# Sums of weight quarters made by accumulating transfers, and paired blocks moved, in the FFNs of a two-block model on one core

## The reference, cut to what matters

```python
x = x + (jax.nn.silu(h2 @ ffn_w1[l]) * (h2 @ ffn_w3[l])) @ ffn_w2[l]
```

## Time and profile before

| | before |
|---|---|
| median of 3 executions | 1043.04 us (1043.03 to 1043.26) |
| span of the profiled execution | 1041.3 us |
| PE busy | 1033.9 us, 99% of the span |
| DVE busy | 843.5 us, 81% |
| ACT busy | 593.8 us, 57% |
| POOL busy | 21.6 us, 2% |
| TensorE's granted clock | full in all 40 slices |

### The profile page before, as it was taken

The page is one execution under the profiler, slowest core; times in us unless marked ns, Lnnn a source line. Parts: engine busy times, 40 slices in busy tenths (PEclk is TensorE's granted clock), DMA queues, the critical chain, the costliest instruction groups (busy, mean ns, idle before and its releaser), DMA issues.

```text
span 1041.3 us, 13328 instructions
## 1 busy us (share of the span) xinstructions
PE 1033.9 (99%) x4884; PEld 841.5 (81%) x4884; DVE 843.5 (81%) x1366; ACT 593.8 (57%) x897; POOL 21.6 (2%) x30
## 2 busy tenths in 40 slices
PE   9999999999999999999999999999999999999998
PEld 7877778888888888788888888787777888888887
DVE  6877889797868987896887788989978878878684
ACT  6845474655646646655656564638656446466462
POOL 0221000000000000000000000000000000000000
PEclk9999999999999999999999999999999999999999
DMA  8762478382456534683743653544444468739243
GB/s 278 228 206 83 128 249 270 122 277 87 142 187 187 180 134 142 216 283 126 246 140 96 221 169 122 158 151 154 147 160 135 148 189 258 242 122 303 85 153 107
DMA packets 135706, 182.97 MB, mean 176 GB/s; under 512 B 12588, under 2 KB 82730, under 8 KB 135514
## 3 DMA queue, kind: packets, MB, share of 16 engines
q1 hardware_dynamic: 134130, 178.36, 53.2%
q0 software_dynamic: 1104, 3.21, 1.2%
q10 hardware_dynamic: 408, 0.56, 0.2%
HBM read 181.03 MB, written 1.05 MB: 175 GB/s over the span
## 4 chain that ended last, share of the span: by engine, by line
PE 92%; DVE 5%; ACT 2%; issue 1%; DVEq 0%; ACTq 0%
PE ps L2169 13%; PE ps L2174 13%; PE ps L2170 13%; PE ps L2186 7%; PE ps L2187 7%; PE ps L2191 7%; PE ps L2309 4%; PE ps L2311 4%; PE ps L2314 4%; PE ps L2152 3%; PE ps L2154 3%; PE ps L2153 3%; DVE wlo L1175 1%; PE ps L2259 1%; PE ps L2242 1%; PE ps L2733 1%
## 5 line engine op out<-in xcount | busy, mean ns | idle before, releaser
L1175 DVE TENSOR_TENSOR wlo<-raw,whi 128x1024 fp32r<-128x1024 f32 (+1 forms) x290 | 349.4, 1232 | 28.8 <-ACT whi L631 27.1
L631 ACT ACTIVATE whi<-raw 128x1024 fp32r<-128x1024 f32 (+1 forms) x290 | 295.5, 1053 | 106.9 <-DMA raw<-in_ffn_w_in 33.1
L2169 PE MATMUL ps<-whi,ath 128*128 128x512 f32 (+1 forms) x688 | 274.5, 400 | 2.2 <-ACT whi L631 0.7
L2170 PE MATMUL ps<-whi,atl 128*128 128x512 f32 (+1 forms) x688 | 266.4, 388 | 0.0
L2174 PE MATMUL ps<-wlo,ath 128*128 128x512 f32 (+1 forms) x688 | 182.9, 388 | 0.0
L2169 PEld LDWEIGHTS ps<-whi,ath 128*128 128x128 f32 x688 | 129.3, 188 | 35.6 <-issue 5.9
L2174 PEld LDWEIGHTS ps<-wlo,ath 128*128 128x128 f32 x688 | 128.2, 188 | 27.4 <-DVE wlo L1175 0.6
L2170 PEld LDWEIGHTS ps<-whi,atl 128*128 128x128 f32 x688 | 129.4, 188 | 24.7 <-issue 0.5
L2186 PE MATMUL ps<-whi,brh 128*128 128x512 f32 x272 | 106.5, 392 | 0.0
L2187 PE MATMUL ps<-whi,brl 128*128 128x512 f32 x272 | 105.9, 389 | 0.0
L1189 DVE TENSOR_TENSOR wlo<-work,whi 128x1024 fp32r<-128x1024 f32 x84 | 98.7, 1220 | 4.5 <-ACT whi L648 4.5
(11 more groups left out here) (380 smaller groups left out, 1415.4 us busy)
## 6 DMA issues: line engine op xcount, KB each, us to landing
raw<-in_ffn_w_in SPq DMA_DIRECT2D x112, 256.0 KB, 3.5
raw<-in_w_in SPq DMA_DIRECT2D x104, 256.0 KB, 2.9
raw<-in_ffn_w SPq DMA_DIRECT2D x100, 256.0 KB, 3.5
raw<-in_ffn_w_out SPq DMA_DIRECT2D x88, 256.0 KB, 3.5
work<-in_ffn_w_in SPq DMA_DIRECT2D x64, 256.0 KB, 4.8
raw<-in_a_w_in SPq DMA_DIRECT2D x48, 256.0 KB, 4.3
raw<-in_b_w_in SPq DMA_DIRECT2D x48, 256.0 KB, 3.1
work<-in_ffn_w SPq DMA_DIRECT2D x32, 256.0 KB, 4.6
```

Source lines behind the costliest of these rows:

```text
L631: a_(unit_view(whi, slot, w), unit_view(raw, slot, w), ACT.Copy).then_inc(hi_ready, 1)
L1175: v_.tensor_tensor(unit_view(wlo, slot, w), unit_view(raw, slot, w), unit_view(whi, slot, w), ALU.subtract).then_inc(lo_ready, 1)
L2169: mm(ps[bk + apart * t][:, 0:w], ath[:, k, t * P:(t + 1) * P], rh[:, kk, :], start=k == 0, stop=False)
L2170: mm(ps[bk + apart * t][:, 0:w], atl[:, k, t * P:(t + 1) * P], rh[:, kk, :], start=False, stop=False)
```

## The change

The pairs move to blocks 5 and 6, and 9 and 10, so the second pair ends the FFN: its last turns and down units take the place of those of the plain block 10, and the turn of one `hid` stands in the middle of the last product. The signs of the scheme change, so that t1 = b11 + b12, t3 = b12 + b22, t2 = b22 + t1 and t4 = b21 + t2; `rneg`, the negative of `rstd`, takes up the sign. DVE makes t2 and t4 only. t1 and t3 are made in their tiles by transfers: one quarter is loaded, and a second transfer adds the other quarter to it (`accum_op`). The quarters are loaded by POOL (`ffn_parts`) in a fixed chain of waits, not by SP: five whole tiles and two added ones a pair, each 4 transfers of 256 KB. The first pair's chain starts at the FFN's second unit, and the second pair's waits tile by tile until the first pair's low halves are made; its last load is b22.

```diff
@@ -56,7 +56,7 @@
-PAIRED = (4, 8)
+PAIRED = (5, 9)
...
@@ -69,8 +69,11 @@
-            plan += [("up", j + 2, c) for c in range(4)]
-            plan += [("down", j + b, k) for b in range(2) for k in range(2)]
+            if j + 2 < FB:
+                plan += [("up", j + 2, c) for c in range(4)]
+                plan += [("down", j + b, k) for b in range(2) for k in range(2)]
+            else:
+                plan += [("down", j, k) for k in range(2)]
...
@@ -87,21 +90,9 @@
-PARTS = [f"{b}_{i}" for b in ("b11", "b12", "b22", "b21") for i in range(2)]
-_p0 = plan_at("pair", 0, "b11", 0)
-PART_LOADS = {}
-for _i, _name in enumerate(PARTS):
-    PART_LOADS.setdefault(6 + 2 * _i, []).append((0, _name))
-for _i, _name in enumerate(PARTS[:4]):
-    PART_LOADS.setdefault(_p0 + 7, []).append((1, _name))
-for _i, _name in enumerate(PARTS[4:]):
-    PART_LOADS.setdefault(_p0 + 18 + _i, []).append((1, _name))
 SUMS = ["a0", "a1", "s1", "s2", "s3", "s4", "l1", "l2", "l3", "l4"]
 for _k in range(len(PAIRED)):
-    SUMS += [f"{_k}_{_t}_{_i}" for _t in ("t1", "t3", "t2", "t4") for _i in range(2)] + [f"{_k}_{_c}" for _c in ("c22", "c11", "c21")]
+    SUMS += [f"{_k}_{_t}_{_i}" for _t in ("t2", "t4") for _i in range(2)] + [f"{_k}_{_c}" for _c in ("c22", "c11", "c21")]
...
@@ -500,14 +494,6 @@
-                    for pair, name in PART_LOADS.get(i, ()):
-                        b, h = name.split("_")
-                        if pair:
-                            sp.wait_ge(lo_ready, u0 + plan_at("pair", 0, "t3" if b == "b12" else b, int(h)) + 1)
-                        block = PAIRED[pair] + (b[2] == "1")
-                        for dst, src in up(pair_part(name), 2 * (b[1] == "2") + int(h), block * 256):
-                            nc.sync.dma_start(dst, src).then_inc(part_loaded[b], 16)
...
@@ -603,6 +589,63 @@
+            def ffn_parts(n, u0, gate_w, gate_n0, up_w, up_n0):
+                gv = gate_w.rearrange("(k p) n -> p k n", p=P)
+                uv = up_w.rearrange("(k p) n -> p k n", p=P)
+                def part(tile, b, j, **how):
+                    for i in range(2):
+                        dst, rows, at = pair_part(f"{tile}_{i}"), 4 * (b[1] == "2") + 2 * i, (j + (b[2] == "1")) * 256
+                        nc.gpsimd.dma_start(dst[:, :, 0:256], gv[:, rows:rows + 2, at + gate_n0:at + gate_n0 + 256], **how)\
+                            .then_inc(part_loaded[tile], 16)
+                        nc.gpsimd.dma_start(dst[:, :, 256:512], uv[:, rows:rows + 2, at + up_n0:at + up_n0 + 256], **how)\
+                            .then_inc(part_loaded[tile], 16)
+                for k, j in enumerate(PAIRED):
+                    def there(name, added=True):
+                        pool.wait_ge(part_loaded[name], parts_there(n, k, name, added))
+                    def free(name):
+                        pool.wait_ge(lo_ready, u0 + plan_at("pair", k - 1, name, 1) + 1)
+                    if k == 0:
+                        pool.wait_ge(unit_used, u0 + 1)
+                        part("t1", "b11", j)
+                        part("b22", "b22", j)
+                        part("t3", "b12", j)
+                        there("t1", False)
+                        part("t1", "b12", j, accum_op=ALU.add)
+                        there("b22")
+                        part("b11", "b11", j)
+                        there("t3", False)
+                        part("t3", "b22", j, accum_op=ALU.add)
+                        there("b11")
+                        part("b21", "b21", j)
+                    else:
+                        free("b11")
+                        part("b11", "b11", j)
+                        free("t3")
+                        part("t3", "b12", j)
+                        free("t1")
+                        part("t1", "b11", j)
+                        there("t3", False)
+                        part("t3", "b22", j, accum_op=ALU.add)
+                        there("t1", False)
+                        part("t1", "b12", j, accum_op=ALU.add)
+                        pool.wait_ge(sem("pair_sums"), sums_done(n, f"{k - 1}_t4_1"))
+                        free("b21")
+                        there("b11")
+                        part("b21", "b21", j)
+                        free("b22")
+                        there("b21")
+                        part("b22", "b22", j)
+            ffn_parts(0, U_F0, D["ffn_w_in"][0], 0, D["ffn_w_in"][0], DFF)
...
@@ -1285,19 +1336,19 @@
+                    if name == "t2":
+                        x0, x1 = "b22", "t1"
+                        dve.wait_ge(part_loaded["b22"], parts_there(n, k, "b22"))
+                        dve.wait_ge(part_loaded["t1"], parts_there(n, k, "t1"))
+                    else:
+                        x0, x1 = "b21", "t2"
+                        dve.wait_ge(part_loaded["b21"], parts_there(n, k, "b21"))
+                        dve.wait_ge(sem("pair_sums"), sums_done(n, f"{k}_t2_{i}"))
+                    v_.tensor_tensor(pair_part(f"{name}_{i}"), pair_part(f"{x0}_{i}"), pair_part(f"{x1}_{i}"), ALU.add)\
...
@@ -1309,19 +1360,8 @@
-                    elif away == 2:
-                        weight_sum(k, "t1", 0)
-                        feed(b + 4)
-                        weight_sum(k, "t1", 1)
-                        feed(b + 5)
-                        turn(j + FB * n)
-                        feed(b + 6)
-                        weight_sum(k, "t3", 0)
-                        feed(b + 7)
-                        hidden(2 * j + 2 * FB * n)
-                        weight_sum(k, "t3", 1)
-                        return
-                    elif away == 1:
+                    elif j + 1 == PAIRED[0]:
+                        k = 0
...
@@ -1359,10 +1399,20 @@
+                    if j + 2 == FB:
+                        turn(j + 1 + FB * n, 2)
+                        hid_of(0, F_part[:, 0, 256:512], hids + 3)
+                        dve.wait_ge(unit_used, b + 16)
+                        part_sum(1, 1)
+                        dve.wait_ge(sem("pair_sums"), sums_done(n, f"{k}_c21"))
+                        hid_of(1, F_part[:, 1, 256:512], hids + 4)
+                        feed(b + 19)
+                        turn(j + 2 + FB * n)
+                        return
...
@@ -1373,19 +1423,19 @@
-                        weight_sum(k + 1, "t1", 0)
+                        weight_sum(k + 1, "t2", 0)
                     feed(b + 20)
                     if more:
-                        weight_sum(k + 1, "t1", 1)
+                        weight_sum(k + 1, "t2", 1)
                     turn(j + 2 + FB * n)
                     feed(b + 21)
                     if more:
-                        weight_sum(k + 1, "t3", 0)
+                        weight_sum(k + 1, "t4", 0)
                     feed(b + 22)
                     hid_of(0, ps[0][:, 256:512], hids + 5)
                     hid_of(1, ps[3][:, 256:512], hids + 6)
                     if more:
-                        weight_sum(k + 1, "t3", 1)
+                        weight_sum(k + 1, "t4", 1)
...
@@ -1396,10 +1446,7 @@
                     else:
                         body(j)
                         j += 1
-                last = u0 + FFN_UNITS - 2
-                feed(last + 2)
-                turn(FB * (n + 1), 2)
-                feed(min(last + 5, U_END))
+                feed(min(u0 + FFN_UNITS + 3, U_END))
             def turns(arg, k, cos, red):
...
@@ -2339,6 +2386,13 @@
+                    if j + 2 == FB:
+                        product(b + 14, 1, *a22, onto=True, middle=lambda: hid_turn(hids + 2))
+                        pe.wait_ge(hid_lo, j + 1 + FB * n)
+                        down_unit((b + 16) % RING, 2, False, False, b + 17, brh, brl)
+                        hid_turn(hids + 4)
+                        down_unit((b + 17) % RING, 3, False, False, b + 18, brh, brl)
+                        return
```

More of the change, by code:

```diff
@@ L281, in build @@
         rhalf = sb("rhalf", [P, 6, NT])
+        rneg = sb("rneg", [P, 6, NT])
         rq_a = sb("rq_a", [P, 64])
@@ L397, in pair_part @@
                      "t1_0", "t1_1", "t2_0", "t2_1", "t4_0", "t4_1")
-            return W(2048 + 1024 * place.index(name.replace("b12", "t3")), 1024).rearrange("p (k n) -> p k n", k=2)
+            return W(2048 + 1024 * place.index(name), 1024).rearrange("p (k n) -> p k n", k=2)
         F_a = W(0, 2048).rearrange("p (k t) -> p k t", k=KT)
@@ L411, in sums_done, with parts_there @@
             return len(SUMS) * n + SUMS.index(name) + 1
-        part_loaded = {"b11": sem("pair_b1_loaded"), "b12": sem("pair_b1_loaded"), "b22": sem("pair_b22_loaded"),
-                       "b21": sem("pair_b21_loaded")}
-        def parts_there(n, k, name):
-            return (128 if name in ("b11", "b12") else 64) * (len(PAIRED) * n + k + 1)
+        part_loaded = {b: sem("pair_whole_loaded") for b in ("b11", "b22", "b21")}
+        part_loaded |= {b: sem(f"pair_{b}_loaded") for b in ("t1", "t3")}
```

(36 more changed lines are left out.)

38 lines of the change are left out of this document (24 added, 14 removed).

## The result

The changed kernel takes 1150.32 us (four executions, 1146.25 to 1153.36) against 1043.08 before: a ratio of 1.1026, with a 95% interval of 1.1002 to 1.1049, 107 us slower. The direction was forecast; the size, 53 us, was half of it, and the range ended at 1138. One execution of a later run (x_plain, 1194 us) was in a slower state of the chip, at a granted clock of 0.84, and is left out of that run's ratio.

A forecast was written before the change was run, and what follows sets the result against it. PE was taken to bound the kernel, busy 1033.9 of 1041.3 us. DVE's wait 43.8, SP's loads 3, FFN end 2.8 and restarts 3 sum to 52.6; on 1043.0 that gives 1096 us, range 1045 to 1138.

The forecast's parts named there:

- DVE's wait for b22, and the restart behind it: Second pair of each FFN: PE waits 14.6 us, 43.8 us over three FFNs, plus 3 us for slow restarts.
- SP's loads beside POOL's: First pair of each FFN: SP's loads lose engine share to POOL's, 0 to 7 us an FFN, 3 us in all.
- the FFN's end: Extra low half before the addition to x, 1.4 us, and a turn inside the last product, 1.4: 2.8 us together.
- What bounds the kernel: Whole kernel: PE, busy 1033.9 of 1041.3 us; removing 29 us of DVE sums is worth nothing, lateness to PE paid in full.
- DVE's wait for the last load: Second pair of each FFN: DVE's sum of t2 waits for b22, so PE waits 14.6 us, 43.8 over three FFNs.
- the working: Second pair's timed chain: t1 free at 206.6, low half done at 241.3, PE waiting 11.75 us; 14.6 taken.
- The first pair's transfers: First pair of each FFN: DVE's sums come in time, SP's loads are slowed; 1 us an FFN taken, 3 in all.
- SP's loads lose half of the engines: Beside the first pair's transfers SP gets 182 GB/s where PE eats 193; 1 us an FFN taken, range 0 to 7.
- Rival 4: Adds cost triple and SP's loads starve 7 us an FFN: 70 + 21 + 6 = 97, 1140 us and up; chance 0.09.
- The restart: After each FFN's long wait PE starts slowly: at most 2.2 us, 1 taken, 3 us over three FFNs.

The follow-up runs named there:

- x_plain: The changed kernel with its adding transfers turned into plain ones of the same size into the same tiles: 1118.96 us, ratio 1.0722.
- x_late: The changed kernel with the second pair's four sums (t2, t4) moved into plain block 8, eight units later, transfers untouched: 1104.48 us, ratio 1.060.
- x_ends: The changed kernel's blocks, signs and FFN end, but SP loads the quarters and DVE makes all eight sums of a pair, as before: 1047.52 us, ratio 1.0040.
- x_late_plain: x_late with plain transfers in place of the adding ones: 1093.04 us, ratio 1.0477.
- x_stall: The kernel before, with DVE making the second pair's first sum of t1 13 times over in each FFN, transfers unchanged: 1084.14 us, ratio 1.0393.

## Why the prediction was wrong, point by point

Four kernels in a row split the 107.2 us; that the parts add up lies in taking differences along a chain:

| step | predicted | measured | by |
|---|---|---|---|
| DVE's wait for b22, and the restart behind it | 43.8 + 3 | 45.8 | changed kernel less x_late |
| SP's loads beside POOL's | 3 | 57.0 | x_late less x_ends |
| the FFN's end | 2.8 | 4.4 | x_ends less before |

The parts are not independent. x_late is rid of the 43.5 us of waits and of 4.3 us of PE's busy time, but PE waits 3.8 us more in its other rows; so 45.8 is the wait and its restart less what starves elsewhere instead. And 57.0 is all that POOL's seven tiles a pair cost beside the ring, adds (some 11 us of it, by x_late_plain) and lower clock included.

**What bounds the kernel: right.** 24 sums fewer (DVE's busy time fell from 843.5 to 816.9) brought nothing, and each lateness was paid.

**DVE's wait for the last load: right in place and mechanism; that the size agrees is luck in part.** The sum of t2 started 38.8 us behind t1's release (237.4 to 276.18), where the working gives about 35; PE came to it 27.2 us behind that release (it ran dry at 264.64), where the working has 22.95, since it had been starved on the way. The two errors, about 4 us each, cancel. x_plain shows the second alone. For plain transfers the working has the sum 32.4 us behind t1's release and a wait of 11.75; in its first FFN the sum starts 31.8 us behind it (233.59 to 265.38), but PE comes late again, and the waits are 4.4 to 7.0. An added transfer was put at 1.5 times a plain one; it is 2.2 times. By the Trainium skill, "Collectives: The Full Stack", Part 3, it would be twice, which is nearer.

**The first pair's transfers: the step that failed.** It was the term "SP's loads lose half of the engines", put at 182 GB/s against the 193 that PE needs, and so at 1 us an FFN with 7 as its end. The row it rested on the earlier trace rows gives halves of the engines' time, for one early stretch, with POOL's packets larger than SP's. I read it as halves of the bytes. (The halves were a mean, too: from 24 to 28 us POOL's packets took 27% and SP's 61%, from 28 to 32 us 92% and 10%.) What the queues share while both have work is turns, one packet each. Beside plain transfers SP's packets are the small ones, and beside added ones all of it is slow; SP got 103 to 134 GB/s, not 182, and the ring ran dry. The same holds behind the products of the first pair, where the working priced only the refill of the ring and no starving at all. Both together are 19 us an FFN, where 1 was taken. In x_late's first FFN PE waits 7.0 us ahead of the first pair and 6.9 in and behind its products, so the two places weigh about the same. Rival 4 (1140 and up) had the starving, and the measured 1150 lies in its range, but by another sum: it had 70 us for DVE's wait and 21 for SP's loads, where the runs give 45.8 and 57.0, and it tied the starving to a triple price of the adds, which wasn't needed: x_late_plain starves without any add.

**What would have shown it before:** the same rows 6. 673 packets carried 1.96 MB and 1372 carried 2.50, 2.9 KB against 1.8 KB a packet; a turn for a turn gives SP's queue 1.8 of each 4.7 KB, 38% of the bytes, not half. (The counts in that stretch are not equal; in its first 4 us POOL's queue has 27 packets to 455 of SP's. When each queue had work there was not traced.)

**The restart: too low.** 1 us each was taken of a bound of 2.2; x_stall has 2.5, most of it by the granted clock, which before's rows couldn't show. By the Trainium skill, "TensorE: Matmul & The Clock Gate", Part 1, the clock falls when PE idles; here the runs agree, with 0.54 behind waits of 11 and 14 us.

**The FFN's end: the mechanism right, the size off.** The extra low half was taken at 0.7 us, and is 1.11 at both ends; the rest, taken at 1.4, is 2.2.

## What to carry to other kernels

Where a second DMA queue is put beside one that feeds the critical engine, price it by packets: in the three stretches read here, where both had work, they got the same number of turns, so beside large packets the queue with small ones gets the small share of the bytes, and beside accumulating packets both are slow. Two fifths of the engines' time left over the span says nothing about a run of 20 us; spread such transfers by the consumer's progress, and ask which load of the other queue is just in time at each place. Work that is taken off an engine which nobody waits for is worth nothing, and a wait that takes its place is paid at once, with some 2.5 us more behind a wait of 11 to 14 us, most of it for the lowered clock.

## What the runs showed of the hardware

An issue on POOL can show a long time and still not hold the queue up. In the timeline of the changed kernel's POOL, the last plain transfer into t1, the first of eight adding ones, the last of them, and a plain one for b21 right behind:

```profile
239.85 0.72 POOL L602 DMA_DIRECT2D work<-in_ffn_w_in  x1
240.57 1.29 POOL L600 DMA_DIRECT2D work<-in_ffn_w_in  x1
...
246.91 3.58 POOL L602 DMA_DIRECT2D work<-in_ffn_w_in  x1
247.64 3.62 POOL L600 DMA_DIRECT2D work<-in_ffn_w_in  x1
```

0.72 us become 3.6, for the plain one too, where in x_plain's first FFN every issue takes 0.72 or 0.73. But the issues overlap: where no wait of the program stands between, the next one starts 0.72 to 0.76 us behind, so no issue is seen to start late for it. The queue's packets differ as well: in the stretch of x_plain above a packet of POOL's has 1.77 MB / 541 = 3.3 KB on the mean, in that of the changed kernel 1.36 MB / 1414 = 1.0 KB.
